# Both directions' diagonal blocks issued in one run, another order of the fill work, a reordered first stage, and constant loads issued by GpSimd

## The chip, the cores and the metric

One core of a Trainium2 chip runs the whole program. The time is the device time of one execution in microseconds; the kernel before took 2563.95 us, the median of three runs (2562.76 to 2565.06).

## The reference

Two blocks of a small sequence model run one behind the other on 256 latent tokens `x` and 256 context tokens (1024 channels, everything fp32). The first block has two layers. The first is an RWKV-7 mixer with 32 heads of 64 and an inner width of 2048, whose state is scanned over the tokens in both directions, the second a Hyena long convolution. The second block has two layers of retention, differential attention and an MLP.

```python
def step(s, inp):                      # per head, once per token, forwards and backwards
    r_t, w_t, k_t, v_t, a_t, b_t = inp
    sa = jnp.einsum('bhvk,bhk->bhv', s, a_t)
    s = s * w_t[:, :, None, :] + sa[..., None] * b_t[:, :, None, :] + v_t[..., None] * k_t[:, :, None, :]
    return s, jnp.einsum('bhvk,bhk->bhv', s, r_t)
...
hx = modulated, normed x               # adaln: three vectors from silu(cond) @ w + b
decay, a = f(tanh(w_lo) @ w2), sigmoid(a0 + a_lo @ a2)      # the "lora" products
filters: hdn = sin(sf * (z @ w1 + b1)), twice more, then filt = hdn @ w4, times a window
```

## The kernel before, in words

The program has two parts with a barrier of all engines between them. Part one (0 to about 1048 us) is the RWKV layer, part two the rest.

**First stage of part one** (`start_sp`, `start_pe`, `start_act`, `start_dve`, `start_pool`). The modulation vectors are a product of the conditioning with 8 MB of weights. SP loads its first half in four steps of 2 MB into two halves of a ring, so step 2 is issued when TensorE has used step 0, and step 3 when it has used step 1 (`mod_used`). TensorE multiplies them (`modulation(0..3)`, 16 instructions each, L248). Between `modulation(2)` and `modulation(3)` stands the sum of squares of x over the channels (L259, 16 instructions of 512 columns), which VectorE needs through `rstd` (ScalarE L317, L319) to scale x (L363). The modulation result is copied out by both engines (L324, L347), transposed (L266), turned into shift and gain, and then ScalarE forms h (L330), VectorE and GpSimd the token shifts and mixes (L339 to L417), and TensorE the low-rank sums (L274, PSUM banks 0 and 1), which ScalarE takes out as `W.low`, with Tanh and Copy, for direction z = 0 and then 1 (L334, L335).

**Pairs.** Sixteen pairs of heads (128 channels) follow, i = 0 to 15. TensorE's order is written out by hand in `pairs_pe`. For pair i it makes the diagonal blocks of both directions (`first_blocks`, L712 and L718, 64 matmul records of 64x64), the full blocks (`full_blocks`, L729), five levels of an inverse by doubling (`below`, L751; `grow`, L766), the solve and the scan of the states. Each of these waits for VectorE, ScalarE or GpSimd, so between them `fill(part, columns)` takes pieces from the generator `between(i)`: the transposes of this pair's keys (`turn_keys`, L613, whose eviction is ScalarE's L1022) and reads (`turn_reads`, L624), and the next pair's projections, one 512-column matmul (two records) per piece (keys L560, values L576, reads L593, gates L602). `fill` takes pieces until the number of columns given (FILL_TOKENS, FILL_MASKS, FILL_BELOW[l], FILL_GROWN[l] and so on) is used up. The lora products `low(m, z)` (L551) of the next pair stand among them: direction 1 may only start when ScalarE has taken direction 0 out of the same banks (`sig[0]`, `rate[0]`, L955, L956). `turn_keys(i, 1, half)` writes the banks that `turn_keys(i, 0, half)` wrote and waits for their eviction (`bk_out[0]`). ScalarE's order in `pairs_act` is: gate sigmoid, both directions' sigmoids, a table load, `squares`, `keys_turned(i, 0, 0)`, `(i, 0, 1)`, `move_inverse(i, 1)`, `keys_turned(i, 1, 0)`, `(i, 1, 1)`, `reads_turned`.

Per pair, with K, V for a piece of keys or values, TK for two key transposes, TR for the transposed reads, B and G for `below` and `grow`, F0 and F1 for the diagonal blocks, X for full blocks and L for a lora product, TensorE's order is F0 L0 F1 X0 L1 TK X1 K B1 TK K G1 K TR K B2 K K G2 ..., and around the last level B5 V seen V G5.

**Part two.** TensorE's `finish_pe` begins with the output projection (L1831), modulation of the next layer (L1760, `modulation_half`) and the filter network (L1870), each layer of which waits for a Sin by ScalarE (L2455). ScalarE issues, behind its first square (`out_square(0, 0)`), five DMAs: `dft`, two halves of `window`, `idft` and `hyena_vec` (2.75 MB; L2449, L2451), then goes on with squares and the Sin of filter layer 1. The windows are first read by VectorE at L2655, `idft` and `hyena_vec` later. GpSimd has nothing to do until the gates (from 1341 us). SP streams weights through a ring of eight 512 KB slots, in the order of use.

Of the kernel before, what the change touches and what calls it, by code (L numbers as in the profile page):

```python
# [20 lines left out]
NX = 256  # L21
# [189 lines left out]
              "silu", "set", "squared", "x_sum", "x_root", "x_scaled", "mod_used", "row_act", "row_dve", "mod_turned", "mod_out",  # L211
              "h_out", "diff_x", "diff_c", "mixed", "low_sum", "low_out")
MIXED_LOW, MIXED_K, MIXED_V, MIXED_R, MIXED_G = 2 * KD, 3 * KD, 4 * KD, 5 * KD, 6 * KD
MOD_ACC, MOD_TURN, X_SUM = 2, 3, 4


def gate_slots(step):
# [22 lines left out]
def start_pe(pe, R, W, s):  # L240
    ps = R.ps

    def modulation(step):
        pe.wait_ge(s[f"mod_loaded{step % 2}"], 64 * (step // 2 + 1))
        for k in (2 * step, 2 * step + 1):
            for q in range(4):
                a = (k % 2) * 512
                mm = pe.matmul(ps[32 * q:32 * q + 4, MOD_ACC, :], R.cond[:, k, :], R.ring[:, 4 * (step % 2) + q, a:a + 512],  # L248
                               start=(k == 0), stop=(k == KD - 1), tile_position=(0, 32 * q))
        mm.then_inc(s["mod_used"], 1)  # L250

    pe.wait_ge(s["silu"], 1)
    for step in range(3):
        modulation(step)
    for k in range(KD):
        pe.wait_ge(s["squared"], k + 1)
        if k == 0:
            pe.wait_ge(s["set"], 1)
        mm = pe.matmul(ps[:, X_SUM, :], R.ones[:, :], R.sq[:, k, :], start=(k == 0), stop=(k == KD - 1))  # L259
    mm.then_inc(s["x_sum"], 1)  # L260
    modulation(3)
    pe.wait_ge(s["const_loaded"], 64)
    pe.wait_ge(s["row_act"], 2)
    pe.wait_ge(s["row_dve"], 2)
    for t in range(4):
        mm = pe.transpose(ps[:, MOD_TURN, t * P:(t + 1) * P], W.rows[:, t * P:(t + 1) * P], R.eye[:, :])  # L266
    mm.then_inc(s["mod_turned"], 1)
    pe.wait_ge(s["low_loaded"], 16)
    wt = R.ring[:, 2:4, :].rearrange("p a (k n) -> p a k n", n=P)
    for k in range(KD):  # L270
        pe.wait_ge(s["mixed"], 2 * k + 2)
        for z in range(2):
            for n, mix in enumerate((W.low_k, W.low_v)):
                mm = pe.matmul(ps[n * 64:n * 64 + 64, z, :], wt[:, n, k, z * 64:z * 64 + 64], mix[:, k, :],  # L274
                               start=(k == 0), stop=(k == KD - 1))
            if k == KD - 1:
                mm.then_inc(s["low_sum"], 1)
# [24 lines left out]
def start_act(act, R, W, I, s):  # L302
# [23 lines left out]
    for k in range(KD):  # L326
        act.wait_ge(s["x_scaled"], k + 1)
        for c in range(2):
            cols = slice(c * NX, (c + 1) * NX)
            act.activation(W.h0[:, k, cols], W.h0[:, k, cols], ACT.Identity, bias=R.mods[:, 0, c, k:k + 1],  # L330
                           scale=R.gain[:, c, k:k + 1]).then_inc(s["h_out"], 1)
    for z in range(2):
        act.wait_ge(s["low_sum"], z + 1)
        act.activation(W.low[0:64, z, :], R.ps[0:64, z, :], ACT.Tanh).then_inc(s["low_out"], 1)  # L334
        act.activation(W.low[64:128, z, :], R.ps[64:128, z, :], ACT.Copy).then_inc(s["low_out"], 1)  # L335


def start_mix(dve, R, W, s, g, dst, k, N):
# [83 lines left out]
ORDER = ([4, 5, 6, 7, 0, 1, 2, 3], [7, 6, 5, 4, 3, 2, 1, 0])  # L422
LAST = 5
FILL_TOKENS = 500
FILL_MASKS = 500
FILL_BELOW = (0, 1000, 1000, 1000, 1000, 500)
FILL_GROWN = (0, 1200, 800, 500, 500, 1000)
FILL_SEEN = 500
FILL_SOLVED = 600
FILL_MOVES = 500  # L430
FILL_STATES = 256
# [100 lines left out]
def pairs_pe(pe, R, W, S, s, Z):  # L532
# [6 lines left out]
    def low(m, z):  # L539
        if z == 0:  # L540
            pe.wait_ge(s["pair_loaded"], 32 * (m + 1))
            if m == 0:
                pe.wait_ge(s["low_out"], 4)
            if m:
                pe.wait_ge(s["r_out"], m)
                pe.wait_ge(s["g_out"], m)
        else:
            pe.wait_ge(sig[0], m + 1)
            pe.wait_ge(rate[0], m + 1)
        for n in range(2):  # L550
            mm = pe.matmul(ps[:, n, :], W.lw[rows(n), m % 2, z, :], W.low[rows(n), z, :], start=True, stop=True)  # L551
        mm.then_inc(low_done[z], 1)
# [91 lines left out]
    def between(i):  # L644
# [4 lines left out]
        for z in range(2):  # L649
# [1 line left out]
                turn_keys(i, z, half)  # L651
                yield 290
            yield key()
        yield key()
        turn_reads(i)
        yield 640
        for _ in range(3):
            yield key()
        if i:
            pe.wait_ge(at_out[1], i + 1)  # L660
# [223 lines left out]
    for i in range(KE):  # L884
        part = between(i) if i < KE - 1 else itertools.chain(between(i), early_pieces())
        first_blocks(i, 0)
        if i + 1 < KE:
            low(i + 1, 0)
        first_blocks(i, 1)
        full_blocks(i, 0)  # L890
        if i + 1 < KE:
            low(i + 1, 1)
# [7 lines left out]
        for l in range(1, LAST + 1):  # L900
# [2 lines left out]
                    pe.wait_ge(t_out[z], (LAST - 1) * i + l - 1)  # L903
            below(l)
            if l == LAST:
                fill(part, FILL_SEEN)
                seen_values(i)
            fill(part, FILL_BELOW[l])
            grow(i, l)
# [1337 lines left out]
def finish_act(act, R, W, I, S, s, layer):  # L2247
# [195 lines left out]
                    act.wait_ge(y["mixed"], len(diff_jobs(l)))  # L2443
                act.activation(W.sig[:, b, 0:NQ], ps[:, 2 * b, 0:NQ], ACT.Sigmoid).then_inc(y["sig"], 1)  # L2444

    window = lambda t: I["window"][:, t].rearrange("p (a n) -> p a n", n=NX)
    out_square(0, 0)
    for dst, src in ((W.dft[:, :, :], I["dft"]), (W.win[0], window(0)), (W.win[1], window(1))):
        act.dma_start(dst, src).then_inc(s["w_loaded"], 16)  # L2449
    for dst, src in ((W.idft[:, :, :, :], I["idft"]), (W.hv[:, :, :], I["hyena_vec"])):  # L2450
        act.dma_start(dst, src).then_inc(s["h_loaded"], 16)  # L2451
    for n in range(3):
        out_square(0, n + 1)
        act.wait_ge(s["f_chain"], 6 * n + 6)
# [619 lines left out]
def finish_pool(pool, R, W, I, S, s, layer):  # L3074
# [9 lines left out]
    def mixing(l):  # L3084
# [3 lines left out]
        pool.dma_start(W.mix_w, I["mlp_w"][l]).then_inc(y["mlp"], 16)  # L3088
        pool.dma_start(W.mix_b, I["mlp_b"][l]).then_inc(y["mlp"], 16)

    for m in range(KE):
        pool.wait_ge(s["gate_out"], m + 1)
        pool.wait_ge(s["taps"], 2 * (2 * KE + m + 1))
# [168 lines left out]
```

## Time and profile before

| | us |
|---|---|
| time, median of 3 | 2563.95 |
| profiled execution: its time, its span | 2570.3, 2568.5 |
| TensorE busy | 2478.8 (97%) |
| VectorE, ScalarE, GpSimd busy | 1180.9, 766.6, 413.7 |
| first `first_blocks` of pair 0, of pair 15, first matmul of part two | 104.3, 972.1, 1049.1 |

An engine's busy time is the sum of stretches in which it has an instruction in flight. Times inside the program are from the start of the span. The span is 1.8 us shorter than the profiled execution's own time, and that execution is 6.35 us longer than the median of the runs.

### The profile page before, as it was taken

What the parts mean: (1) busy time and instruction counts of PE and PEld (TensorE: products, weight loads), DVE (VectorE), ACT (ScalarE), POOL (GpSimd) and SP (SyncE); (2) the same over time, 40 slices, a digit from 0 to 9 for tenths busy, and PEclk for the clock granted to TensorE, in tenths of its full rate; (3) what the DMA queues carried; (4) which work ended last, traced back from release to release, by engine and by line L of the source; (5) the groups of instructions that cost most, each with busy time, mean ns of one, the idle gap of its engine ahead of it and who ended that gap; (6) DMA issues with size and microseconds to landing.
All of it is one profiled execution on the core that took longest, in us unless ns stands there. A gap on an engine that the chain in (4) does not pass through costs nothing.

```text
span 2568.5 us, 62194 instructions
## 1 busy us (share of the span) xinstructions
PE 2478.8 (97%) x27332; PEld 1652.7 (64%) x27332; DVE 1180.9 (46%) x2455; ACT 766.6 (30%) x1527; POOL 413.7 (16%) x441
## 2 busy tenths in 40 slices
PE   5999999999999998799999999999999999999998
PEld 1466667666666676568888864446544458775787
DVE  3766666666666664454563333204611114442512
ACT  2444444454544542131220220003400014102301
POOL 2344343334444341000001000000000000000000
PEclk8999999999999998899999999999999999999999
DMA  6211111111111104545447632220244444441343
GB/s 244 89 45 38 45 39 46 46 38 38 38 48 38 46 20 167 183 141 154 132 132 262 219 107 74 76 72 29 68 142 137 129 127 143 126 131 62 94 151 104
DMA packets 81891, 258.08 MB, mean 100 GB/s; under 512 B 11639, under 2 KB 19160, under 8 KB 80856
## 3 DMA queue, kind: packets, MB, share of 16 engines
q1 hardware_dynamic: 75304, 242.94, 29.3%
q10 hardware_dynamic: 5712, 8.02, 0.9%
q8 instruction: 219, 3.59, 0.6%
q0 software_dynamic: 608, 3.15, 0.4%
q14 instruction: 48, 0.39, 0.0%
HBM read 253.02 MB, written 1.05 MB: 99 GB/s over the span
## 4 chain that ended last, share of the span: by engine, by line
PE 56%; DVE 2%; ACTq 1%; ACT 0%; issue 0%; DVEq 0%
PE ps L1961 13%; PE ps L2129 10%; PE ps L1906 9%; PE ps L1831 7%; PE ps L2146 5%; PE ps L1991 4%; PE ps L2033 2%; PE ps L1760 1%; PE ps L2053 1%; PE ps L2018 1%; PE ps L2073 1%; PE ps L2012 1%; PE ps L1939 1%; PE ps L1927 1%; ACTq L2451 0%; PE ps L2063 0%
## 5 line engine op out<-in xcount | busy, mean ns | idle before, releaser
L1961 PE MATMUL ps<-h,ring 128*128 128x256 f32 (+1 forms) x1184 | 358.9, 465 | 0.0
L1961 PEld LDWEIGHTS ps<-h,ring 128*128 128x128 f32 x1184 | 225.0, 190 | 132.6 <-issue 114.3
L2129 PE MATMUL ps<-h,ring 128*128 128x512 f32 (+1 forms) x768 | 256.0, 486 | 0.0
L1906 PE MATMUL ps<-h,ring 128*128 128x256 f32 x1024 | 225.6, 379 | 0.0
L1906 PEld LDWEIGHTS ps<-h,ring 128*128 128x128 f32 x1024 | 193.9, 190 | 34.9 <-issue 9.9
L2129 PEld LDWEIGHTS ps<-h,ring 128*128 128x128 f32 x768 | 145.0, 190 | 101.7 <-issue 91.8
L1032 ACT ACTIVATE general<-general 64x512 f32<-64x512 f32 x160 | 101.8, 636 | 162.9 <-DVE general L1231 160.3
L560 PE MATMUL ps<-general,ring 128*128 128x512 f32 x256 | 134.9, 623 | 0.8 <-issue 0.8
L576 PE MATMUL ps<-general,ring 128*128 128x512 f32 x256 | 134.1, 629 | 0.6 <-issue 0.6
L2146 PE MATMUL ps<-general,ring 128*128 128x512 f32 (+1 forms) x384 | 131.0, 486 | 0.0
L751 PEld LDWEIGHTS ps<-general 64*64 64x64 f32 (+1 forms) x5120 | 77.8, 130 | 73.0 <-issue 49.3
L2444 ACT ACTIVATE general<-ps 128x512 f32<-128x512 f32 (+1 forms) x48 | 23.2, 490 | 329.4 <-PE ps L2129 329.4
L3088 POOL DMA_DIRECT2D general<-in_mlp_w x2 | 1.1, 548 | 710.0 <-DVE general L2823 710.0
L1991 PE MATMUL ps<-ring,h 128*128 128x512 f32 x256 | 110.2, 592 | 0.0
L2754 DVE COPY general<-ps 128x256 f32<-128x256 f32 (+1 forms) x50 | 25.7, 520 | 183.8 <-PE ps L1961 183.8
L2942 DVE TENSOR_TENSOR general<-ps,general 128x512 f32<-128x512 f32 (+1 forms) x32 | 17.9, 558 | 199.7 <-PE ps L2146 199.7
L2146 PEld LDWEIGHTS ps<-general,ring 128*128 128x128 f32 x384 | 73.0, 190 | 50.9 <-issue 45.9
L1831 PE MATMUL ps<-general,ring 128*128 128x256 f32 x456 | 103.0, 384 | 2.5 <-PEq L78 2.5
L1231 DVE STREAM_TRANSPOSE general<-general 128x512 f32<-128x512 f32 x160 | 104.3, 691 | 2.2
L1831 PEld LDWEIGHTS ps<-general,ring 128*128 128x128 f32 x456 | 86.1, 191 | 24.2 <-issue 11.0
L766 PEld LDWEIGHTS ps<-general 64*64 64x64 f32 x4096 | 66.8, 136 | 50.1 <-issue 49.0
L751 PE MATMUL ps<-general 64*64 64x32 f32 (+1 forms) x5120 | 86.5, 216 | 12.0 <-DVE general L1204 7.9
(369 smaller groups left out, 4091.3 us busy)
## 6 DMA issues: line engine op xcount, KB each, us to landing
ring<-in_w_mods SPq DMA_DIRECT2D x96, 512.0 KB, 5.6
ring<-in_w_feature SPq DMA_DIRECT2D x74, 512.0 KB, 3.5
ring<-in_w_rkvg SPq DMA_DIRECT2D x64, 512.0 KB, 3.7
ring<-in_w_in SPq DMA_DIRECT2D x48, 512.0 KB, 3.6
ring<-in_w_merge SPq DMA_DIRECT2D x48, 512.0 KB, 3.5
ring<-in_w_out SPq DMA_DIRECT2D x32, 512.0 KB, 6.3
ring<-in_w_token SPq DMA_DIRECT2D x24, 512.0 KB, 3.7
ring<-in_w_merge SPq DMA_DIRECT2D x48, 256.0 KB, 3.0
```

Of the source, the lines that this page charges most:

```text
L560: mm = pe.matmul(ps[:, 0, :], W.wt[:, 0, k, :], W.mix_k[:, k, :], start=(k == 0), stop=(k == KD - 1))
L576: mm = pe.matmul(ps[:, 1, :], W.wt[:, 1, k, :], W.mix_v[:, k, :], start=(k == 0), stop=(k == KD - 1))
L751: mm = pe.matmul(ps[own, b0 + h, j * P:j * P + 32], left, right, start=True, stop=True)
L766: mm = pe.matmul(ps[a:a + 64, b0 + h, j * P:j * P + 32], W.U[g:g + 64, z, q, :], W.Y[g:g + 64, z, q, :], start=True, stop=True)
L1032: last = act.activation(W.U[g:g + 64, 1], W.X0[a:a + 64, 1], ACT.Copy)
L1231: dve.transpose(out, W.T[:, z]).then_inc(done, 1)
L1831: mm = pe.matmul(ps[:, dense_bank(n), 0:NX], weights(key, k % 8), rhs(k), start=(k == 0), stop=(k == K - 1))
L1906: mm = pe.matmul(ps[:, n % 4, 0:NX], weights(key, k), R.h[:, k, 0:NX], start=(k == 0), stop=(k == KD - 1))
L1961: mm = pe.matmul(ps[:, feature_bank(l, j), 0:width], weights(("feature", l, j), k), R.h[:, k, cols], start=(k == 0), stop=(k == KD - 1))
L1991: mm = pe.matmul(ps[:, feature_bank(l, GAP + n), :], R.h[:, k, t * P:(t + 1) * P], weights(("token", l, g, k // 2), k % 2, 512), start=(k ...
L2129: mm = pe.matmul(ps[:, 2 * b, 0:NQ], weights(key, k), R.h[:, k, 0:NQ], start=(k == 0), stop=(k == KD - 1))
L2146: mm = pe.matmul(ps[:, 2 * b + 1, 0:NQ], weights(key, k), W.F[:, 4 * (RG, MG, DG)[b] + k, 0:NQ], start=(k == 0), stop=(k == KB - 1))
```

## The change

TensorE's order per pair becomes F0 F1 L0 X0 L1 TK X1 K TK B1 K TR G1 K K B2 K K G2 ..., and around the last level B5 seen V V G5. ScalarE, VectorE and GpSimd keep their order in the pairs. In the first stage the sum of squares stands behind `modulation(0)`, the low-rank sums have banks 5 and 6, `low(0, 0)` waits for direction 0 alone, and a table set is named ahead of the Tanh. The five constant loads of part two go from ScalarE to the head of GpSimd's program.

```diff
-MOD_ACC, MOD_TURN, X_SUM = 2, 3, 4
+MOD_ACC, MOD_TURN, X_SUM, LOW_SUM = 2, 3, 4, 5
@@ start_pe
-    for step in range(3):
-        modulation(step)
+    modulation(0)
     ...  (the sum of squares)
-    modulation(3)
+    for step in range(1, 4):
+        modulation(step)
@@ start_act  (reads and writes of the low-rank sums go to bank LOW_SUM + z)
+    act.preload_act_table_set("sigmoid_and_others")
     for z in range(2):
@@
-FILL_MASKS = 500
-FILL_BELOW = (0, 1000, 1000, 1000, 1000, 500)
-FILL_GROWN = (0, 1200, 800, 500, 500, 1000)
-FILL_SEEN = 500
+FILL_MASKS = 900
+FILL_BELOW = (0, 1000, 1000, 1000, 1000, 1000)
+FILL_GROWN = (0, 1000, 800, 500, 500, 1000)
@@ low(m, z)
-            if m == 0:
-                pe.wait_ge(s["low_out"], 4)
...
+        if m == 0:
+            pe.wait_ge(s["low_out"], 2 * z + 2)
@@ between(i)
-        yield key()
         turn_reads(i)
         yield 640
-        for _ in range(3):
+        for _ in range(4):
             yield key()
@@ pairs_pe
         first_blocks(i, 0)
+        first_blocks(i, 1)
         if i + 1 < KE:
             low(i + 1, 0)
-        first_blocks(i, 1)
@@
             if l == LAST:
-                fill(part, FILL_SEEN)
                 seen_values(i)
@@ finish_act -> finish_pool
-    for dst, src in ((W.dft[:, :, :], I["dft"]), (W.win[0], window(0)), (W.win[1], window(1))):
-        act.dma_start(dst, src).then_inc(s["w_loaded"], 16)
-    for dst, src in ((W.idft[:, :, :, :], I["idft"]), (W.hv[:, :, :], I["hyena_vec"])):
-        act.dma_start(dst, src).then_inc(s["h_loaded"], 16)
+    (the same two loops with pool.dma_start, ahead of all else that GpSimd does in part two)
```

## Rows read from the trace of the kernel before

**Rows 1.** Windows: busy us per engine (instructions), TensorE's granted clock, DMA share, GB/s

```profile
240.00:310.00 70.00, 69.45 (x1676) 47.52 (x1676) 45.35 (x93) 32.46 (x61) 32.13 (x34) 1.00 0.15 45
25.60:29.10 3.50, 3.50 (x16) 0.41 (x16) 0.00 (x0) 0.00 (x0) 0.00 (x0) 0.50 0.99 387
1070.80:1074.30 3.50, 3.50 (x18) 0.38 (x17) 2.61 (x7) 0.42 (x1) 0.00 (x0) 0.50 0.33 112
```

**Rows 2.** Timeline of the first stage: start us, us, what, idle before

```profile
19.84 1.90 PE L248 MATMUL ps<-ring,cond 128*4 128x512 f32 x16 [2.04 <-DMA ring<-in_w_mods]
...
25.59 3.60 PE L248 MATMUL ps<-ring,cond 128*4 128x512 f32 x16 [3.85 <-DMA ring<-in_w_mods]
...
29.12 8.29 PE L259 MATMUL ps<-sq,ones 128*128 128x512 f32 x16
...
38.83 4.91 DVE L363 TENSOR_TENSOR general<-x,rstd 128x512 f32<-128x512 f32 x8 [38.83 <-ACT rstd L319]
...
43.77 1.42 DVE L347 COPY general<-ps 4x512 f32<-4x512 f32 x2
```

**Rows 3.** Timeline, the end of the low-rank sums and the first lora products

```profile
67.74 0.59 ACT L334 ACTIVATE general<-ps 64x512 f32<-64x512 f32 x1
...
69.09 1.13 PE L551 MATMUL ps<-general 64*128 64x512 f32 x4 [1.76 <-ACT general L335]
...
70.30 1.28 ACT L955 ACT_TABLE_LOAD   x1 [1.35 <-PE ps L551]
...
73.00 1.13 PE L551 MATMUL ps<-general 64*128 64x512 f32 x4 [0.97 <-ACT sq L956]
```

**Rows 4.** Timeline, start of part two

```profile
1053.44 7.17 PE L1831 MATMUL ps<-general,ring 128*128 128x256 f32 x32
...
1055.27 11.14 ACTq L2451 DMA_DIRECT2D general<-in_idft  x1
...
1069.68 1.12 PE L1870 MATMUL ps<-general 64*64 64x256 f32 x4 [9.07 <-ACT general L2455]
...
1088.45 1.29 DVE L2655 TENSOR_TENSOR general<-ps,x 128x512 f32<-128x512 f32 x2
```

**Rows 5.** SP's issues of w_mods from 1053.5 to 1053.9 us

```profile
DMA to landing us min/median/max: 7.3/8.0/8.7
```

**Rows 6.** SP's issues of w_out at 1054.6 and 1055.1 us

```profile
DMA to landing us min/median/max: 9.6/10.3/10.9
```

**Rows 7.** TensorE's waits, 110 to 1020 us: who for whom, total us, times, longest

```profile
PE ps L751 <- DVE general L1204: 7.9, 16, 1.5
```

**Rows 8.** TensorE's timeline in pair 5

```profile
394.81 0.69 PE L712 MATMUL ps<-general 64*64 64x64 f32 x32
...
395.90 1.13 PE L551 MATMUL ps<-general 64*128 64x512 f32 x4
...
399.05 1.03 PE L551 MATMUL ps<-general 64*128 64x512 f32 x4
...
402.12 1.12 PE L560 MATMUL ps<-general,ring 128*128 128x512 f32 x2
403.67 1.14 PE L751 MATMUL ps<-general 64*64 64x32 f32 x64 [0.43 <-DVE general L1204]
...
411.97 1.98 PE L560 MATMUL ps<-general,ring 128*128 128x512 f32 x4
```

**Rows 9.** ScalarE's timeline in the same pair

```profile
397.71 0.68 ACT L956 ACTIVATE sq<-ps,general 128x512 f32<-128x512 f32 x1
...
403.02 1.07 ACT L1022 ACTIVATE general<-ps 128x512 f32<-128x512 f32 x2
404.18 1.29 ACT L1032 ACTIVATE general<-general 64x512 f32<-64x512 f32 x2
```

**Rows 10.** TensorE's timeline in pair 15, which has no lora product

```profile
972.10 0.69 PE L712 MATMUL ps<-general 64*64 64x64 f32 x32
...
974.13 1.16 PE L729 MATMUL ps<-general 64*128 64x128 f32 x16
```

More of the change, by code:

```diff
@@ L273, in start_pe @@
             for n, mix in enumerate((W.low_k, W.low_v)):
-                mm = pe.matmul(ps[n * 64:n * 64 + 64, z, :], wt[:, n, k, z * 64:z * 64 + 64], mix[:, k, :],
+                mm = pe.matmul(ps[n * 64:n * 64 + 64, LOW_SUM + z, :], wt[:, n, k, z * 64:z * 64 + 64], mix[:, k, :],
                                start=(k == 0), stop=(k == KD - 1))
@@ L331, in start_act @@
                            scale=R.gain[:, c, k:k + 1]).then_inc(s["h_out"], 1)
+    act.preload_act_table_set("sigmoid_and_others")
     for z in range(2):
         act.wait_ge(s["low_sum"], z + 1)
-        act.activation(W.low[0:64, z, :], R.ps[0:64, z, :], ACT.Tanh).then_inc(s["low_out"], 1)
-        act.activation(W.low[64:128, z, :], R.ps[64:128, z, :], ACT.Copy).then_inc(s["low_out"], 1)
+        act.activation(W.low[0:64, z, :], R.ps[0:64, LOW_SUM + z, :], ACT.Tanh).then_inc(s["low_out"], 1)
+        act.activation(W.low[64:128, z, :], R.ps[64:128, LOW_SUM + z, :], ACT.Copy).then_inc(s["low_out"], 1)
 def start_mix(dve, R, W, s, g, dst, k, N):
@@ L2444, in sigmoids @@
                 act.activation(W.sig[:, b, 0:NQ], ps[:, 2 * b, 0:NQ], ACT.Sigmoid).then_inc(y["sig"], 1)
-    window = lambda t: I["window"][:, t].rearrange("p (a n) -> p a n", n=NX)
     out_square(0, 0)
-    for dst, src in ((W.dft[:, :, :], I["dft"]), (W.win[0], window(0)), (W.win[1], window(1))):
-        act.dma_start(dst, src).then_inc(s["w_loaded"], 16)
-    for dst, src in ((W.idft[:, :, :, :], I["idft"]), (W.hv[:, :, :], I["hyena_vec"])):
-        act.dma_start(dst, src).then_inc(s["h_loaded"], 16)
     for n in range(3):
@@ L3089, in mixing @@
         pool.dma_start(W.mix_b, I["mlp_b"][l]).then_inc(y["mlp"], 16)
+    window = lambda t: I["window"][:, t].rearrange("p (a n) -> p a n", n=NX)
+    for dst, src in ((W.dft[:, :, :], I["dft"]), (W.win[0], window(0)), (W.win[1], window(1))):
+        pool.dma_start(dst, src).then_inc(s["w_loaded"], 16)
+    for dst, src in ((W.idft[:, :, :, :], I["idft"]), (W.hv[:, :, :], I["hyena_vec"])):
+        pool.dma_start(dst, src).then_inc(s["h_loaded"], 16)
     for m in range(KE):
```

## The prediction

> **What bounds the kernel now.** I began with the windows. In a steady stretch of the pairs TensorE is busy 69.45 of 70 us at a granted clock of 1.00, while VectorE has 45, ScalarE 32 and the DMA 15% [rows 1]. So the pairs are a string of TensorE instructions, and an edit there is worth what it takes out of TensorE's string: waits, and the price of changing between shapes. TensorE's waits came next: from 110 to 1020 us one alone recurs, once in each pair, that of the first level (B1) for VectorE's masks, 7.9 us over 16 pairs [rows 7]. Then the timelines of the three places that the diff touches outside the steady loop. In the first stage TensorE is not the bound: it idles for weights (2.04 and 3.85 us) and the sum of squares runs only at 29.12 us, so that VectorE scales x from 38.83 and copies its modulation rows at 43.77, behind that [rows 2]. At the first lora products ScalarE paces the work [rows 3]. In part two ScalarE's queue is held 11.14 us by the issue of one DMA, and TensorE idles 9.07 us for a Sin that stands behind it [rows 4]. The sum is made in the profiled execution (2570.3 us); the median of the runs is 6.35 us lower, and I carry the difference over.
>
> **First stage, up to h.** The sum of squares moves behind modulation(0), which ends at 19.84 - 2.04 = 17.8. Its 16 instructions of 512 columns took 8.29 us, the first of them at half clock; at full clock one takes 0.43, by the key pieces (1.98 for four, 1.12 for two, overlapped) [rows 8], 6.9 in all. I take 7.7, so it ends at 25.5. Steps 1 and 2 of the weights are there by 19.84 and 25.59 [rows 2], so modulation(1) and (2) follow at 1.90 each, to 27.4 and 29.3. But SP issues step 3 only when modulation(1) is done, 27.4 where it was 21.7 (19.84 + 1.90). Step 2 was issued at 17.8 and had landed at 25.59, 7.8 us with another step ahead of it in the queue; step 3 has an empty queue, and I take 7.4: 34.9. The wait of 5.6 us is longer than the 3.85 after which the granted clock was 0.50 and the same product took 3.60 [rows 1, 2], so modulation(3) ends at 38.5. Before, it ended at 39.2 (29.12 + 8.29 + 1.90, less overlap). This end is thus hardly earlier; what changes is VectorE. Its scaling of x (4.91 us) now runs at about 27 to 32 and is long over, so it copies the rows at 38.6 instead of 43.77. All that leads to h (transposes, shift, gain) hangs on that copy: 5.1 us earlier. Bounds: nothing, if step 3 landed 5 us later than I have it; 6.8, if modulation(3) ran warm.
>
> **First stage, low-rank sums.** low(0, 0) waits for direction 0's two evictions, not all four: two of 0.6 us [rows 3] less, 69.09 becomes 67.85. It is over at 69.0, when ScalarE is free (67.74 and two evictions: 68.9). The table load of 1.28 us at 70.30, between that product and the first sigmoid, goes if the named set serves Tanh too; both evictions of the product would then end at 70.4 instead of 72.9. TensorE's own string is the later limit for low(0, 1): it was idle for 0.97 ahead of it [rows 3], so the gate product in between ended at 72.03, now at 70.8. low(0, 1) moves from 73.00 to 70.8: 2.2 us, and keys, mixes and the rest of the stage follow. Bounds 1 (table load stays) to 2.6. First stage together: -7.3.
> The row shows the load start only when the product has ended, and take 1.28 us; the second product, which waits for both evictions, starts at 73.00, and 1.28 and two evictions of 0.7 fill that time but for 0.1 [rows 3]. The Trainium skill (ScalarE: Activation LUTs, "Table sets: the hidden batching unit") lists tanh in the sigmoid set, by which the load does go; the same page, under "What ACT_TABLE_LOAD costs", gives a switch as the load plus a drain of about 1.4 us. By that the gain in ScalarE's string would be 1.4 larger, but by those times the trace has no room for it here, and TensorE's 0.97 of idle time caps it in any case.
>
> **Pairs, what is taken out.** A switch between shapes has a price. Two diagonal blocks next to each other took 974.13 - 972.10 = 2.03 us [rows 10]; apart, each took 1.09 (395.90 - 394.81) [rows 8], 2.18 in all: -0.15. Two key pieces in one run took 1.98, two separate ones 2 x 1.12 [rows 8]: -0.26. The new order has one such merge around the last level (V V for V, seen, V), one of the transposed reads with G1 and, for it, one key run less. I take -0.15 for the diagonal blocks, -0.3 for the reads beside G1 and -0.25 for the last level: -0.7 per pair. The wait of B1 (7.9/16 = 0.5; in this pair 0.43) [rows 7, 8] goes too, since two transposes now stand ahead of B1.
>
> **Pairs, what is put in.** Both new places wait for ScalarE. (1) L0 now starts after both diagonal blocks, at 394.81 + 2.03 = 396.84 instead of 395.90. ScalarE ends taking it out 2.49 us after its start (397.71 + 0.68 - 395.90) [rows 8, 9], so direction 1 may start at 396.84 + 2.49 + 0.1 = 399.43. With the full blocks behind L0 (about 1 us each) TensorE would be there at 398.8: a stall of 0.6, and L1 ends up 0.4 later than before (399.05), the merge counted. (2) TK of direction 1 needs the eviction of direction 0's transposes. ScalarE begins that 3.97 us after L1 (403.02 - 399.05) and needs 1.07 for both halves [rows 9], behind its sigmoids, a table load and a square; that string hangs on L1, so it moves with it. TensorE arrives 3.07 (X1 to K: 402.12 - 399.05) + 0.9 = 4.0 us after L1; the first half is out at +4.6, the second at +5.1. B1 then starts at about L1 + 5.65, where without the wait it would be +4.9: a stall of 0.7 in place of 0.43. Queued behind it is all of TensorE; VectorE is ahead and has slack. (3) The transposed reads need the second eviction, which stands behind ScalarE's move of the inverse (1.29 us, from 404.18) [rows 9]. Both now end late: first half out, second out, the move, then two more evictions of 1.07 together, L1 + 5.1 + 1.3 + 1.1 = +7.5; TensorE gets there after B1 and K, at L1 + 5.65 + 2.1 = +7.75. No stall, but by 0.2 only.
> Sum per pair: +0.4 (L1, diagonal merge counted) + 0.7 - 0.43 - 0.3 - 0.25 = +0.1, over 15 pairs +2 us. Bounds from the same rows: if ScalarE were in time everywhere, -0.7 - 0.43 = -1.1 per pair, -17 us; if the third wait opened as well and merges gave nothing, +1 per pair, +15. Pair 15 has no lora product and is paced by VectorE: 0 (within 1 us).
>
> **Part two.** With the issue gone from ScalarE, the Sin follows VectorE's steps at once, while TensorE is still in its projection, and the next filter layer can go when its projection ends, 1053.44 + 7.17 = 1060.6 [rows 4], not at 1069.68. What is late next is the DMA: the modulation weights that follow landed at 1053.9 + 8.7 = 1062.6 [rows 5] and the two halves of the projection behind them at 1064.2 and 1066.0 [rows 6]. So TensorE waits to 1062.6 where it had waited to 1070.8: 8.2. It is also warmer: the product at 1070.8 ran at a granted clock of 0.50 for 3.5 us [rows 1], where 1.9 is its time at full clock [rows 2]: 1.6. Together 9.8. Against it: GpSimd issues all 2.75 MB from 1049, some 2 us ahead of ScalarE's issues and without their pauses, and takes bandwidth from the very weights that now set the pace; at 390 GB/s [rows 1] the 4 MB of weights and 2.75 MB of constants need 17.3 us from 1049, the same end as 1066.0, with the middle up to 2 us later. I take -9.3, bounds -3 and -11 (what follows at half clock before, about 0.8, gained too).
> On this the Trainium skill (DMA: Bandwidth & Descriptors, "Issuing engines are not separate DMA queues") says that another issuing engine saves only the sequencer's time, usually small. Here that time is 11.14 us and on the chain [rows 4], so the trace goes the other way on "small", while its first half is why I count landing times.
>
> **Sum.** -7.3 + 2 - 9.3 = -14.6: 2570.3 becomes 2555.7, and the median 2563.95 becomes 2549.3.
>
> **The rivals.**
> (a) ScalarE's waits don't open, and the pairs gain 1.1 us each: ScalarE has 32 of 70 us busy [rows 1], so half a microsecond might be found. Against it, both waits hang on strings of instructions without gaps [rows 9]. 2549.3 - 2 - 17 = 2530; with half of it, 2539.
> (b) Part two gives little: the weights land later, because GpSimd's constants are ahead of them in the shared DMA engines. Gain 3: 2556.
> (c) The first stage gives nothing up to h, step 3 of the weights being the new bound: 2554.
> (d) GpSimd's descriptors are written late and the constants land after their first use, at about 1079 in the new time (1088.45 less 9.3) [rows 4]. That leaves 30 us from 1049, where bandwidth alone asks for 17. If it overran by 10 us the gain of part two would be gone: 2559. The Trainium skill (same page, "SWDGE vs HWDGE vs iDMA") gives the way: GpSimd writes descriptors into SBUF and VectorE can lock it out. VectorE has long gaps there, and no row shows GpSimd issuing in such company.
> (e) Slower: the stalls on ScalarE in the pairs (L1 and TK) are paid and the third one, of the transposed reads, opens behind them, because each ScalarE string starts from the stalled product before it. It decides from 1.5 us per pair (the other gains, 16.6, plus the 5.1 that can be told, over 15 pairs). With 0.6 + 0.7 + 0.5 of stalls, merges worth nothing it is 1.8 per pair, +27: 2549.3 - 2 + 27 = 2574. For it speaks the margin of 0.2; against it, it needs a second 0.5 that no row shows.
>
> **How the numbers follow.** Forecast 2549 with its own range 2543 to 2554: 0.57. (a) 0.20, (b) 0.07, (c) 0.07, (d) 0.05, (e) 0.04. Below 2534 lies about a third of (a), above 2558 (e) and a part of (d): range 2534 to 2558. A measurement of this kernel tells 0.2%, 5.1 us, from no change, so faster means below 2558.8: all but (e) and part of (d), 0.91; same 0.05; slower 0.04.
>
> **What would show it.** First stage: VectorE's row copy near 38.6, h from 42, first diagonal block of pair 0 near 97 instead of 104.3; modulation(3) waits for a DMA and takes 3.6. Pairs: L0 2.0 after F0, L1 waiting about 0.6 for ScalarE (L956), the second TK about 0.7 for L1022, no wait of B1 for L1204, a period of 57.7 us against 57.6. Part two: no issues on ScalarE, the second filter layer at 11.5 us from TensorE's first matmul there instead of 20.6, then a wait of 1 to 4 us for w_mods. I am wrong if the period moves by more than 0.5 us either way, or if the filter products wait for the windows.

## The result and the profile after

The changed kernel takes 2570.81 us (median of 12 runs, 2567.32 to 2574.60), the kernel before beside it 2564.43 (12 runs). The ratio is 1.0027 with a 95% interval of 1.0019 to 1.0034: slower by 0.3%, where 2549.3 was forecast. The profiled execution has a span of 2572.8 us against 2568.5 before, so the two traces differ by +4.3 us, and three sections of them account for that. (Both are single executions above their medians: this one, 2574.6 us, is the slowest of the twelve.)

```
first stage, to pair 0's first diagonal block:       104.3 -> 96.4              -7.9  (forecast -7.3)
pairs, from there to part two's first matmul:        944.8 -> 960.9            +16.1  (forecast +2)
part two, its start to the third filter layer:       33.06 -> 29.17             -3.9  (forecast -9.3)
```

The page of the changed kernel has TensorE's busy sum, the queue of GpSimd's issues (q0) and the one that fetches code (q8); a queue's columns are packets, MB and share of 16 engines:

```profile
PE 2479.7 (96%) x27332; PEld 1659.3 (64%) x27332; DVE 1181.5 (46%) x2455; ACT 765.0 (30%) x1526; POOL 407.5 (16%) x446
...
q0 software_dynamic: 1360, 5.89, 0.6%
...
q8 instruction: 219, 3.59, 0.6%
```

The windows of the changed kernel (columns as in [rows 1]) show a steady stretch of pairs and the two stretches at half clock:

```profile
240.00:310.00 70.00, 67.78 (x1662) 46.43 (x1654) 43.89 (x88) 33.38 (x64) 31.70 (x34) 1.00 0.14 43
...
35.00:38.60 3.60, 3.56 (x16) 0.41 (x16) 0.00 (x0) 0.00 (x0) 0.00 (x0) 0.50 1.01 398
1074.90:1078.50 3.60, 3.56 (x17) 0.48 (x17) 0.00 (x0) 0.00 (x0) 0.00 (x0) 0.50 1.03 398
```

TensorE is now idle for 2.2 of 70 us in this stretch of pairs, where it was idle for 0.55 [rows 1], at a clock that is full in both. So the loss of this stretch is not one of the clock; in two other pairs it partly is, as shown below. TensorE's waits in the pairs name part of it (who for whom, total us, times, longest); "issue" is a wait in which the profile shows no releaser:

```profile
PE ps L551 <- ACT sq L954: 8.9, 14, 0.9
PE ps L613 <- ACT general L1020: 5.2, 13, 0.4
PE ps L789 <- issue: 3.8, 5, 1.8
PE ps L750 <- issue: 2.2, 2, 1.6
PE ps L624 <- ACT general L1020: 1.8, 1, 1.8
...
PE ps L750 <- DVE general L1202: 0.5, 1, 0.5
```

B1's wait for the masks, 7.9 us before [rows 7], is down to 0.5 (last line). L1's wait for ScalarE (first line, 0.64 each) and the key transposes' (second line, 0.40 each) stand in its place. The timeline of pair 5 shows both at their places, to be held against [rows 8] (the L numbers of the two kernels differ by a few lines):

```profile
390.33 0.69 PE L711 MATMUL ps<-general 64*64 64x64 f32 x32
...
392.37 1.13 PE L551 MATMUL ps<-general 64*128 64x512 f32 x4
393.33 1.06 PE L728 MATMUL ps<-general 64*128 64x128 f32 x16
395.00 1.13 PE L551 MATMUL ps<-general 64*128 64x512 f32 x4 [0.61 <-ACT sq L954]
...
399.70 1.15 PE L613 MATMUL ps<-eye,general 128*128 128x128 f32 x8 [0.40 <-ACT general L1020]
400.78 1.14 PE L750 MATMUL ps<-general 64*64 64x32 f32 x64
```

L0 starts 2.04 after F0 (forecast 2.03) and L1 4.67 after it (forecast 4.62). The transposes stall by 0.40 (forecast 0.7, as TensorE gets there 4.3 after L1 and not 4.0), and B1 starts at L1 + 5.78 (forecast 5.65). So the two stalls that I predicted are there and at their places, the first in its size and the second at little over half of it. To see what is left I split each of the 15 pairs at the starts of the same steps; below are medians over the pairs, their sum, and the sum of the 15 periods as they are. What the second exceeds 15 times the first by is irregular: stalls that only some pairs have.

```
                  F0-L1 L1-B1 B1-G1 G1-B2 B2-B5 B5-G5 G5-F0   sum   15 x sum  15 periods  irregular
before             4.24  4.63  2.95  4.27 16.14  3.89 21.44  57.56    863.4      867.8       4.4
changed            4.66  5.78  3.10  2.97 16.14  3.93 21.44  58.02    870.3      883.5      13.2
diagonal_only      4.66  4.73  2.95  4.27 16.14  3.89 21.45  58.09    871.4      876.7       5.3
masks_only         4.24  5.69  3.10  2.98 16.14  3.89 21.44  57.48    862.2      867.6       5.4
changed_low_back   4.24  5.68  3.10  2.97 16.14  3.92 21.44  57.49    862.4      867.9       5.5
```

The loss in the pairs is 15.7 us: 6.9 regular (0.46 a pair, forecast 0.1) and 8.8 irregular (forecast: no such term). Of the irregular part 7.4 us lie in two steps. These are F0 to L1 and B5 to G5 in pairs 0 to 14, the stalls in brackets:

```
F0-L1 before    4.24 [5.95] 4.24  4.24  4.24  4.24  4.24  4.24  4.24  4.24  4.24  4.24  4.24  4.24  4.24
F0-L1 changed   4.66 [6.42] 4.66 [5.24] 4.66  4.68 [5.66] 4.66  4.66 [5.49] 4.66 [5.19][5.10] 4.66  4.66
B5-G5 before    4.25  3.89  3.89 [4.73] 3.89  3.89  3.89  3.89  3.89  3.89 [4.77] 3.89  3.89  3.92  3.89
B5-G5 changed   3.78  3.96  3.83 [4.70][4.37] 3.83  3.92 [7.59] 3.83  3.92 [5.48] 3.94  4.05  3.84  3.93
```

The largest, in pair 7 at the last level, in TensorE's timeline:

```profile
541.25 1.00 PE L789 MATMUL ps<-general 64*64 64x64 f32 x51
544.02 0.45 PE L789 MATMUL ps<-general 64*64 64x64 f32 x13 [1.78 <-issue]
544.41 3.68 PE L576 MATMUL ps<-general,ring 128*128 128x512 f32 x4
```

It cuts one helper's run of 64 small products in two, behind 64 small ones of the last level (540.43), and no engine is waited for. In these 10 us (538 to 548) the DMA moved nothing but code, one of the two packets from 541.30 to 542.69 us:

```profile
q8 instruction: 2, 0.03, 1.6%
```

The stall ends at 544.02, 1.33 us after that packet. This is so throughout. Code packets come about every 5.5 us in the pairs (162 from 100 to 1000 us). The changed kernel has 12 waits without a releaser in that time, and the ten of 0.27 us or longer end as follows (us):

```
end of a q8 packet   156.94 272.81 305.45 365.13 449.51 542.69 628.41 720.84 746.49 995.17
end of the stall     158.27 274.32 306.89 366.48 451.12 544.02 629.97 722.40 747.90 996.63
difference             1.33   1.51   1.44   1.35   1.61   1.33   1.56   1.56   1.41   1.46
```

In the 13 traces of this case together there are 98 such waits; 92 of them, with all 78 of 0.25 us or longer, end 1.2 to 1.7 us after a code packet has ended. Of the 263 waits for an engine in the same time 6 do. What ends such a stall is thus the arrival of the next piece of the program. (That is read from the traces; no experiment changed the arrival itself.)

The stall has a second price. The four products behind it take 3.68 us, where four of the same in pair 5, at 425.24 us, take 1.98, since the granted clock is down to half:

```profile
425.24 1.98 PE L576 MATMUL ps<-general,ring 128*128 128x512 f32 x4
...
544.50:547.80 3.30, 3.30 (x4) 1.05 (x4) 0.00 (x0) 2.23 (x4) 0.00 (x0) 0.50 0.02 5
```

The clock is at half for 3.4 us here and again from 158.8 us, behind the stall of 1.71 us in pair 1; in the kernel before it is full from 55 to 980 us. I estimate from the steps of these two pairs that it makes 3 of the 8.8 irregular us (1.7 here, about 1.4 in pair 1).

The first stage ran as forecast; to be held against [rows 2]:

```profile
17.18 7.93 PE L258 MATMUL ps<-sq,ones 128*128 128x512 f32 x16
25.04 3.62 PE L248 MATMUL ps<-ring,cond 128*4 128x512 f32 x32
35.05 3.60 PE L248 MATMUL ps<-ring,cond 128*4 128x512 f32 x16 [6.39 <-DMA ring<-in_w_mods]
...
38.78 1.42 DVE L348 COPY general<-ps 4x512 f32<-4x512 f32 x2 [7.35 <-PE ps L248]
```

In part two the Sin no longer holds TensorE (the filter layer L1868 at 1068.73 has no wait, against 9.07 us [rows 4]), but the modulation weights do:

```profile
1057.32 1.97 PE L1829 MATMUL ps<-general,ring 128*128 128x256 f32 x8 [2.45 <-PEq L78]
...
1061.63 7.17 PE L1829 MATMUL ps<-general,ring 128*128 128x256 f32 x32
1068.73 0.65 PE L1868 MATMUL ps<-general 64*64 64x256 f32 x4
1074.94 3.59 PE L1758 MATMUL ps<-ring,cond 128*4 128x512 f32 x16 [5.56 <-DMA ring<-in_w_mods]
```

That product starts 17.6 us after part two's first matmul. Before it was 21.7 (1070.80 - 1049.13), though its weights had landed at 13.5 [rows 5]. The traffic of its first 20 us tells why they are late. Of the kernel before (1049 to 1069), SP's queue and ScalarE's:

```profile
q1 hardware_dynamic: 1440, 5.24, 70.3%
q10 hardware_dynamic: 1585, 1.72, 25.0%
...
ring<-in_w_mods SPq DMA_DIRECT2D x4, 512.0 KB, 7.7
```

and of the changed kernel (1057 to 1077), SP's queue and GpSimd's:

```profile
q1 hardware_dynamic: 1125, 4.13, 55.7%
q0 software_dynamic: 749, 2.74, 38.3%
...
ring<-in_w_mods SPq DMA_DIRECT2D x4, 512.0 KB, 9.9
```

Both moved nearly 7 MB in 20 us; 1.0 MB more of it was constants, and the weights got 1.1 MB less.

### The profile page after: what moved, and what is told of

It reads as the page before. It is cut to its first block, busy times and chain, and to the rows that moved or that the text cites. A ratio compares the mean times of both kernels' runs of the same rounds, so it can differ in the third digit from the quotient of the medians.

```text
span 2572.8 us, 62193 instructions
## 1 busy us (share of the span) xinstructions
PE 2479.7 (96%) x27332; PEld 1659.3 (64%) x27332; DVE 1181.5 (46%) x2455; ACT 765.0 (30%) x1526; POOL 407.5 (16%) x446
## 3 DMA queue, kind: packets, MB, share of 16 engines
q8 instruction: 219, 3.59, 0.6%
HBM read 253.02 MB, written 1.05 MB: 99 GB/s over the span
## 4 chain that ended last, share of the span: by engine, by line
PE 56%; DVE 1%; DMA 0%; ACT 0%; issue 0%; DVEq 0%; SPq 0%; ACTq 0%
PE ps L1959 13%; PE ps L2127 10%; PE ps L1904 9%; PE ps L1829 7%; PE ps L2144 5%; PE ps L1989 4%; PE ps L2031 2%; PE ps L1758 1%; PE ps L2051 1%; PE ps L2016 1%; PE ps L2071 1%; PE ps L2010 1%; PE ps L1937 1%; PE ps L1925 1%; PE ps L1890 1%; DMA ring<-in_w_mods 0%
## 5 line engine op out<-in xcount | busy, mean ns | idle before, releaser
L1904 PEld LDWEIGHTS ps<-h,ring 128*128 128x128 f32 x1024 | 193.9, 190 | 34.9 <-issue 9.9
```

The costliest lines, as they stand in the source:

```text
L1904: mm = pe.matmul(ps[:, n % 4, 0:NX], weights(key, k), R.h[:, k, 0:NX], start=(k == 0), stop=(k == KD - 1))
```

## Experiments

All are edits of the kernel before unless it says "changed kernel". Each ratio is against the kernel before, run beside it.

**start_only**: the diff's edits to the first stage alone.

```diff
-    for step in range(3):
-        modulation(step)
+    modulation(0)
...
+    for step in range(1, 4):
+        modulation(step)
...
+    act.preload_act_table_set("sigmoid_and_others")
```

> The kernel before with the first stage's edits alone (sum of squares behind modulation(0), own banks for the low-rank sums, the named table set). Theory A (the change's parts add up, each where it stands): the first diagonal block of pair 0 at 96.4 us instead of 104.3, the pairs and part two as before, so 7.9 us faster, 2556.5 beside 2564.4. Rival B (an earlier stage is given back: the pairs run into a later wait, or the clock is lower afterwards): the pairs' mean period rises above 57.9 us and the total gains less than 5 us.

Measured: 2558.70, ratio 0.9967 (0.9954 to 0.9979), -7.8 us; pair 0's first diagonal block at 97.5, where 96.4 was expected. The gain is real and nothing gives it back later. One trace fixes this stage to about 1 us only: the block stands at 96.4 to 97.5 in the six traces with the new stage, and at 102.3 to 104.8 in the seven with the old one.

**loads_only**: the constants issued by GpSimd, nothing else.

```diff
-    for dst, src in ((W.dft[:, :, :], I["dft"]), (W.win[0], window(0)), (W.win[1], window(1))):
-        act.dma_start(dst, src).then_inc(s["w_loaded"], 16)
...
+        pool.dma_start(dst, src).then_inc(s["w_loaded"], 16)
```

> The kernel before with the five constant loads of part two issued by GpSimd at its head, nothing else. Theory A: 3.9 us faster; the third filter layer's matmul comes 29.2 us after part two's first matmul instead of 33.1, and TensorE waits some 5.6 us for w_mods, which land about 17.6 us after the start of part two instead of 13.5, since the constants now take their share of the DMA engines from the first microsecond. Rival B (the late weights in the changed kernel were an accident of that execution, the loads alone give the 9.3 us of the prediction): the weights land by 14 us and the gain is 8 to 10 us. Rival C (software-issued loads cost time elsewhere, in VectorE or later loads): gain under 2 us.

Measured: 2564.04, ratio 0.9991 (0.9980 to 1.0001), -2.4, which is not clear of noise by itself; the third filter layer 29.23 us into part two against 33.06. A good 3.8 us in the trace, and of my 9.3 no more.

**diagonal_only**: both diagonal blocks ahead of L0.

```diff
         first_blocks(i, 0)
+        first_blocks(i, 1)
         if i + 1 < KE:
             low(i + 1, 0)
-        first_blocks(i, 1)
```

> The kernel before with the one edit that both directions' diagonal blocks stand ahead of the next pair's first lora product. Theory A (the lora product of direction 1 waits for ScalarE): L1 starts 4.67 us after F0 instead of 4.24, the period rises by 0.42 us in a pair without disturbance, 6.3 us over 15 pairs. Theory A2 (on top of it, 128 small matmuls in one run outrun the supply of instructions): some pairs have 0.5 to 1.0 us more between the diagonal blocks and L0, with no engine to wait for, 3 us in all, so 9 us slower in sum. Rival B (a run of one shape is cheaper, and ScalarE's later start is absorbed by B1's old wait for VectorE of 0.43): no change, within 2 us.

Measured: 2577.23, ratio 1.0040 (1.0027 to 1.0052), +10.7. It costs more by itself than the whole change does. Its waits show L1's new one, and that B1's stays:

```profile
PE ps L551 <- ACT sq L956: 8.6, 14, 0.6
PE ps L751 <- DVE general L1204: 7.9, 16, 1.5
```

**seen_only**: the last level's fill in front of `seen_values` moved behind it.

```diff
-FILL_BELOW = (0, 1000, 1000, 1000, 1000, 500)
+FILL_BELOW = (0, 1000, 1000, 1000, 1000, 1000)
...
-                fill(part, FILL_SEEN)
```

> The kernel before with the value piece between the last level and seen_values moved behind seen_values, nothing else (two value pieces in one run there). The prediction priced this at -0.25 us per pair, -4 us (rival B). Theory A (two groups of 64 small matmuls side by side give nothing back, and at times run out of instructions): B5 to G5 takes 3.93 us in an undisturbed pair, as before (3.89), and 0.5 to 2 us more in three or four pairs, so 2 to 4 us slower in sum.

Measured: 2569.00, ratio 1.0007 (0.9997 to 1.0017), +2.5: the timing is inconclusive. In the trace the step from B5 to G5 has the median 3.93 (3.89 before) and the 15 periods sum to 867.8, as before. The -0.25 that I had taken for it is not there. The changed kernel has the same edit, and its pair 5, beside that of the kernel before (the first two lines), shows why:

```profile
427.05 0.76 PE L751 MATMUL ps<-general 64*32 64x32 f32 x64
427.73 1.12 PE L576 MATMUL ps<-general,ring 128*128 128x512 f32 x2
...
423.33 0.76 PE L750 MATMUL ps<-general 64*32 64x32 f32 x64
424.15 1.16 PE L789 MATMUL ps<-general 64*64 64x64 f32 x64
```

The two value pieces in one run do save 0.2: from start to start 1.91 instead of 1.06 + 1.05. But B5 has lost its large neighbour, and directly ahead of the 64 small products of `seen_values` it takes 0.82 instead of 0.68, and in ten of the changed kernel's 15 pairs the step loses another 0.09 us or more.

**masks_only**: the key piece and the fills around B1.

```diff
-FILL_MASKS = 500
+FILL_MASKS = 900
-FILL_GROWN = (0, 1200, 800, 500, 500, 1000)
+FILL_GROWN = (0, 1000, 800, 500, 500, 1000)
...
-        yield key()
         turn_reads(i)
         yield 640
-        for _ in range(3):
+        for _ in range(4):
```

> The kernel before with the fill order around the first two levels alone (K and both transposes of direction 1 ahead of B1, the transposed reads next to G1, two key pieces behind G1). Theory A: in an undisturbed pair L1 to B2 takes 11.99 us instead of 11.85, as in the changed kernel: the wait for ScalarE's L1022 (0.4, and about 0.15 more inside the transposes) replaces B1's 0.43 for VectorE, and the two merges give 0.1; 2 us slower over 15 pairs, 0 to 4. Rival B (prediction's price of merges, -0.3 per pair, holds and something else slowed that stretch): -0.4 to -3 us.

Measured: 2566.99, ratio 1.0006 (0.9997 to 1.0014), +1.6. Its regular sum is 0.08 a pair below before's; L1 to B2 takes 11.77 against 11.85, where I had expected 11.99. The timing is inconclusive; by the trace one wait is exchanged for another (0.40 for 0.43), and the new neighbours earned under a tenth of a microsecond: the key pieces and the reads save 0.2, but direction 1's transposes, now directly ahead of B1, take 1.08 instead of 0.93.

**late_loads**: loads_only, and GpSimd waits for the second filter layer first, so that the weights are ahead of the constants.

```diff
+    pool.wait_ge(s["f_layer"], 2)
     for dst, src in ((W.dft[:, :, :], I["dft"]), (W.win[0], window(0)), (W.win[1], window(1))):
         pool.dma_start(dst, src).then_inc(s["w_loaded"], 16)
```

> The kernel before with the five constant loads issued by GpSimd, but only when TensorE has done the second filter layer, about 11.5 us into part two. Theory A (in the changed kernel the constants' 2.75 MB took DMA time from the weights that TensorE waits for): w_mods land by 11 us into part two instead of 17.6, TensorE waits under 1 us for them, the third filter layer's matmul comes at 21 to 23 us instead of 29.2 (33.1 before): 10 to 12 us faster than the kernel before. The windows are first read at about 28 us and have landed by 22. Rival B (the weights are late because SP issues them late): the third filter layer stays at 29. Rival C: the windows come too late and VectorE's first product waits, gain 5 us.

Measured: 2553.70, ratio 0.9963 (0.9950 to 0.9975), -11.7. Its timeline has no wait for weights, and the modulation product runs at full clock:

```profile
1059.71 0.65 PE L1870 MATMUL ps<-general 64*64 64x256 f32 x4
1060.29 1.90 PE L1760 MATMUL ps<-ring,cond 128*4 128x512 f32 x16
1062.12 7.17 PE L1831 MATMUL ps<-general,ring 128*128 128x256 f32 x32
1069.23 0.65 PE L1870 MATMUL ps<-general 64*64 64x256 f32 x4
```

The third filter layer comes 22.39 us into part two, 10.7 earlier than before. The price is one wait of VectorE for a window, 1.0 us. Against loads_only, with the same issues on the same engine, one wait is worth 9.3 us by the medians: the order in which the DMAs enter the shared engines was what failed in part two.

**turns_first**: diagonal_only, and the key transposes of direction 0 ahead of L1, so that L1 need not wait.

```diff
-        if i + 1 < KE:
-            low(i + 1, 1)
         fill(part, FILL_TOKENS)
+        if i + 1 < KE:
+            low(i + 1, 1)
```

> The kernel before with both diagonal blocks in one run ahead of the lora product, as in the change, and the second lora product (L1) moved behind the two key transposes. Theory A (the change's loss at this place is L1's wait of 0.6 us for ScalarE, and nothing else): L1 has no wait, the period in an undisturbed pair is 57.2 to 57.5 us instead of 58.0 with L1 in its old place and 57.55 before; the total is within 3 us of the kernel before. Rival B (the run of 128 small matmuls itself costs): pairs still lose 0.3 to 1 us between the diagonal blocks and L0 in some pairs, 3 us in sum or more; the period's mean stays over 58.

Measured: 2567.53, ratio 1.0012 (1.0003 to 1.0021), +2.1. In pair 5 L1 waits for nothing:

```profile
395.37 1.06 PE L729 MATMUL ps<-general 64*128 64x128 f32 x16
396.36 1.09 PE L613 MATMUL ps<-eye,general 128*128 128x128 f32 x8
397.38 1.13 PE L551 MATMUL ps<-general 64*128 64x512 f32 x4
```

Undisturbed pairs take 57.39 to 57.45, less than the 57.56 of before, so that most of diagonal_only's cost was L1's wait. But TensorE's waits with no releaser (100 to 1000 us) are 10.0 us against 6.8 before (of which 3.8 and 3.3 stand in pair 15), with 0.4 to 0.7 each in pairs 6, 9 and 12 between F0 and L0, the very pairs in which diagonal_only has them too, and the kernel is still not faster.

**changed_shifted**: the changed kernel, with 32 small matmuls into an unused tile at TensorE's start, so that all its later instructions lie that much further on.

```diff
+            pe.wait_ge(s["set"], 1)
+            for _ in range(32):
+                pe.matmul(R.ps[:, 7, 0:4], R.ones[:, :], R.ones[:, 0:4], start=True, stop=True)
             start_pe(pe, R, W, s)
```

> The changed kernel with 32 tiny matmuls (4 columns, on constants, into a bank that is free) at the head of TensorE's program, where TensorE waits for its first weights anyway: 128 more instructions, half of one 16 KB piece of the instruction queue. Theory A (the irregular stalls of 0.5 to 2 us behind runs of small matmuls are the fetch of the next 16 KB piece of instructions falling into such a run): the stalls move to other pairs or other places of the pair than in the changed kernel (there: between diagonal blocks and L0 in pairs 3, 6, 9, 11; behind seen_values in 4, 7, 10), the sum over 15 pairs may change by 5 us either way. Rival B (they come from ScalarE or VectorE being late in certain pairs): the same pairs and places.

Measured: 2572.03, ratio 1.0037 (1.0025 to 1.0049). The stalls that recur (L1, transposes) stay; those with no releaser move, most of them, to other pairs (F0 to L1 in 1, 2, 5, 7, 10 and 12 instead of 1, 3, 6, 9, 11 and 12; B5 to G5 in 0, 3, 10, 11 and 14 instead of 3, 4, 7 and 10) and grow from 9.5 to 12.9 us (100 to 1000 us). This is not chance of one execution: loads_only and late_loads have the TensorE program of the kernel before, and their irregular stalls stand in its pairs 1, 3 and 10 again. So they hang on where an instruction lies in the program, not on what the pair computes.

**changed_low_back**: the changed kernel, with L0 back between the two diagonal blocks.

> The changed kernel with the first lora product back between the two diagonal blocks, all else as changed. Theory A (that edit is the largest loss, by L1's wait for ScalarE and by the run of 128 small matmuls; alone it cost 10.7 us): 9 to 11 us faster than the changed kernel, so 3 to 6 us faster than the kernel before. Rival B (the changed pairs' loss comes from the fill order, the diagonal edit shares it): under 5 us faster than the changed kernel, so not faster than the kernel before.

Measured: 2559.97, ratio 0.9980 (0.9971 to 0.9988): 10.8 us below the changed kernel, and faster than before by 5.2. Its waits keep the transposes' and have lost L1's; of those without releaser 4.5 us are left where the changed kernel has 9.5:

```profile
PE ps L613 <- ACT general L1020: 5.7, 14, 0.4
PE ps L789 <- issue: 2.0, 4, 1.4
```

So it is this one edit that turns the change from faster to slower. In the table above the move costs 15.6 us here: 7.9 regular, and 7.7 of irregular stalls (by itself it had 5.3 against 4.4 before). By the medians it is 11.6 (+6.4 against -5.2): the traces are of the slowest execution of the one kernel and the fastest of the other, so some 4 us of the difference may be of these two executions alone.

**start_and_late**: start_only and late_loads together.

> The kernel before with the first stage's edits and the constant loads issued by GpSimd after the second filter layer; the pairs as before. If the places are independent, -7.8 and -11.7 add up to -19.5 us, a ratio of 0.9924. Rival (the gains share a cause, as a cooler stretch of clock or a common wait): under 15 us.

Measured: 2549.28, ratio 0.9938 (0.9926 to 0.9951), -15.9 where -19.5 would be the sum of the two medians. The interval is 12.6 to 19.0 us: the full sum lies just outside it and the rival's range (under 15) reaches into it. So that the two gains add up in full is not shown.

**start_late_keyrun**: the same, and a key piece between the key transposes of both directions, so that ScalarE is in time for the second, with B1 a little later.

```diff
-FILL_MASKS = 500
+FILL_MASKS = 1000
-FILL_GROWN = (0, 1200, 800, 500, 500, 1000)
+FILL_GROWN = (0, 1100, 800, 500, 500, 1000)
...
+            if z == 0:
+                yield key()
             yield key()
```

> As start_and_late, and in the pairs two key pieces in one run ahead of B1, with direction 1's transposes still behind B1. Theory A: B1's wait for VectorE (0.43) is covered by work that waits for nobody, and two key pieces in one run save another 0.1 to 0.2: 0.5 us per undisturbed pair, period 57.0 to 57.1, 7 to 8 us faster than start_and_late. Rival B (something in that stretch follows later, as the transposed reads waiting for ScalarE behind later transposes): no change against start_and_late.

Measured: 2539.49, ratio 0.9901 (0.9886 to 0.9917), -25.7, of which the key pieces bring 9.8 (expected 7 to 8). B1 waits for nobody and the period is 56.7 to 57.1 in 11 of the 15 pairs:

```profile
388.35 1.16 PE L732 MATMUL ps<-general 64*128 64x128 f32 x16
389.44 1.99 PE L561 MATMUL ps<-general,ring 128*128 128x512 f32 x4
391.35 1.14 PE L754 MATMUL ps<-general 64*64 64x32 f32 x64
392.42 1.09 PE L614 MATMUL ps<-eye,general 128*128 128x128 f32 x8
```

This kernel beats both: what the change wanted with B1 is to be had if the wait is covered with a run of large products, and not passed to ScalarE.

## Why the prediction was wrong

- **First stage: right.** -7.9 in the trace and -7.8 by start_only's median against -7.3. Modulation(3) at 35.05 (forecast 34.9), the row copy at 38.78 (38.6). Of the -7.9, 5.0 were there at the row copy (43.77 before, forecast 5.1); the other 2.9 stand against 2.2 for the low-rank sums.
- **Stalls in the pairs: right in place.** L1 0.61 (forecast 0.6) and the transposes 0.40 (forecast 0.7), B1's wait gone. L1 to B2 is 11.85 as before, forecast -0.03, and that agreement is luck: a stall 0.3 too large made up for merges that were 0.3 too large. The third stall opened in pair 15 alone (1.8 us), so rival (e) is not how the kernel became slower, though its sign was right.
- **Merges in the pairs: the step that failed first.** Of -0.7 a pair, the diagonal blocks' -0.15 is in the 2.04 us of F0 to L0. The -0.25 of the last level is +0.04 (seen_only the same), and the -0.3 of the reads beside G1 is -0.1 at most (masks_only: 0.08 below before, with its stalls of 0.40 in and 0.43 out). Two things were wrong. The merges of key and value pieces were priced by durations (1.98 against 2 x 1.12), which overlap the next instruction; from start to start it is 0.2 (under seen_only). And a piece that leaves its place makes new neighbours: B5 ahead of `seen_values` and the transposes ahead of B1 each cost 0.15, for which the sum had no term. Regular sum +0.46 instead of +0.1: 5 us.
- **A cost with no term: irregular stalls, 8.8 us.** My sum took TensorE to have its next instruction always at hand. In pairs 0 to 14 it lost 3.4 us by waits without a releaser before (6 of them) and 7.8 now (11); pair 15 has 3.3 and 1.6 more. The rest is inside groups, which the waits do not list, and in the two stretches at half clock, some 3 us. The waits end 1.2 to 1.7 us after a code packet has landed, changed_shifted shows that they hang on the program's position, and changed_low_back and turns_first that they are more where small products stand side by side. All of it points to the supply of TensorE's instructions as the cause, though no experiment changed that supply by itself. Why the move brings 7.7 us of irregular loss in the changed kernel and 0.9 by itself stays open.
- **Part two: rival (b), at 0.07, was the case.** The Sin and its 9.07 us went, as forecast. The weights came 17.6 us after TensorE's start and not at 13.5: I had left their landing where [rows 5] has it. ScalarE's slow issues (11.14 us for one [rows 4]) had kept the constants back, to the weights' good; GpSimd's five issues went out in 3.7 us. The 1.6 us at half clock, which I had as gained, stayed as well (3.59 at 0.50 above), since the wait before it did. late_loads gives the forecast gain back in full: -10.7 in part two's trace, -11.7 by the medians.
  On this the Trainium skill (DMA: Bandwidth & Descriptors, "Issuing engines are not separate DMA queues") says that DMAs run on the same 16 engines and interleave whichever engine started them. The runs agree: the median landing of the weights went from 7.7 to 9.9 us with GpSimd's queue at 38.3% of the engines. I had cited it, and then priced its consequence at 0.5 us (9.8 to 9.3); it was 4.1 by the later landing and 1.6 by the clock.
- **The sum.** Single parts by their medians: -7.8 -2.4 +10.7 +2.5 +1.6 = +4.6; all together +6.4. Within the noise of five medians the change is additive. The error of 21.5 us (2570.81 - 2549.3) is, by the traces, 14.1 in the pairs and 5.4 in part two, less 0.6 in the first stage; the remaining 2.6 is the step from the profiled execution to the medians. The range was 2534 to 2558, too narrow for it: both its ends were built from waits, and none from the supply of instructions or from what new neighbours cost.

## What to carry to other kernels

Before a DMA leaves a slow issuing engine, ask what its slowness held back: here one wait in front of the moved loads turned -2.4 us into -11.7. A wait is best covered by moving large independent work ahead of it; trading it for a wait on another engine (masks_only) earns nothing, and a gain by "fewer switches of shape" is to be read from start to start, and set against what the pieces cost beside their new neighbours. Judge a reordering by the median of each step and by the sum over all repeats: single stalls in some repeats can be more than the regular part, and they move when anything ahead of them changes length.

## What the runs showed of the hardware

- TensorE has stalls with no releaser, 0.2 to 3.9 us long, and 92 of 98 in 13 traces end 1.2 to 1.7 us after a packet of its code queue (q8: 219 packets of 16 KB in the changed kernel) has ended. Most moved to other pairs when 32 matmuls were put ahead of the program. Their total from 100 to 1000 us was 4.5 to 12.9 us in kernels that do the same work.
- Behind a stall of 1.78 us in a stretch at full clock the granted clock was 0.50 for 3.4 us, and four products took 3.68 instead of 1.98 us. Stalls of 1.3 us in the kernel before and 1.84 us in turns_first left it at 1.00.
- From start to start a product of 512 columns (two records) took 1.05 to 1.06 us beside small groups, and two in a row took 1.91; 64 products of the last level took 0.68 ahead of a large one and 0.82 ahead of 64 small ones.
- One issue on ScalarE took 11.14 us [rows 4] (its other four took 0.34 to 3.20), where five by GpSimd, of the same data, went out from 1057.79 to 1061.5 us (0.58 to 0.94 each). These are two of them, in the changed kernel:

```profile
1058.54 0.94 POOL L3086 DMA_DIRECT2D x<-in_window  x1
...
1060.33 0.58 POOL L3088 DMA_DIRECT2D general<-in_idft  x1
```

- Rival (d), late descriptors, did not come: the last of the constants landed 17.3 us after its issue, and the second window at 1076, ahead of its first reader at 1092.75.
- After idle times of 6.39 and 5.56 us TensorE's clock was granted at 0.50, and the same product took 3.6 instead of 1.9 us; with no idle time ahead of it (late_loads) it ran at 1.90.
